# A float32 decoder layer on one core: feed-forward products from GpSimd to VectorE, compressed scores 64 columns wide, and other orders on VectorE and ScalarE

## Chip, core and metric

The kernel runs on one core of a Trainium2 chip. The metric is the time of one execution on the device in microseconds (us); the number compared is the median over runs. All arithmetic is float32 in and out. Where a matrix product needs full precision, each operand is split in two parts, `hi` (rounded to the fp32r form) and `lo` (the rest), and three fp32r products are added: lo by hi, hi by lo, hi by hi.

## What is computed

One decoder layer over 512 tokens of width 2048. The reference, cut to what matters:

```python
h = rms_norm(x, norm_mix)
proj = h @ w_in + b_in                       # q, k, v of two head groups, gates
# group A, 16 heads, three branches, mixed by sigmoid gates:
kc, vc = compress(k_c), compress(v_c)        # 31 compressed tokens per kv head (4 kv heads)
s_c = q @ kc.T * scale + bias;  p_c = masked_softmax(s_c);  o_c = p_c @ vc
o_s = attention over selected blocks         # here all 8 blocks: causal attention
o_w = attention over a window of 512
o_a = g0 * o_c + g1 * o_s + g2 * o_w
# group B, 16 heads: window of 128, one sink per head
x = x + concat(o_a, o_b) @ w_out
h = rms_norm(x, norm_ffn)
x = x + (silu(h @ w_gate) * (h @ w_up)) @ w_down      # width 5632
return rms_norm(x, norm_final)
```

## The kernel before

Each engine has its own instruction stream, written out by hand; engines wait for each other with counting semaphores (`pe.wait_ge(masked, n)` and the like), and the order within an engine is the order of the code. SyncE issues nearly all DMAs.

**Front, to about 230 us.** x is transposed, squared and split; `w_in` comes in units of 2048 columns through a ring. ScalarE makes the hi part of a unit (`split_hi`), VectorE the lo part (`split_lo`, line 1681), TensorE multiplies.

**Attention, about 230 to 600 us.** The work is a list of items: `c` is the compressed branch of two heads, `s` and `w` are the selected and the window branch of one head, `b` is a head of group B. There are 8 `c` items. The loop goes over x, and in step x TensorE does `score(x)`, `transpose_first(x-2)`, small pieces of `w_in` that fill the time (`mini`, lines 2876 to 2880), `transpose_third(x-2)` (line 2754) and `products(x-3)` (line 2784). VectorE adds the bias to the scores of x (`mask_scores`, line 1943, for `c` items lines 1911 to 1918), normalises x-1 (line 1977), makes lo parts of minis (1746), makes lo parts of the stacked queries and keys of the next round of four heads (`stack_lo_of`, line 1893, three steps of each round), and copies a third of the transposed probabilities of x-2 out of PSUM (`copy_third`, line 1987). `transpose_first` of a later step waits for that copy. In a `c` item TensorE makes 16 matmuls of 32 columns: for each of 4 token tiles and 2 heads one with `kc_lo` (line 2695) and one with `kc_hi` (2697), added up in PSUM. Item x+1 writes its fourth tile to bank 0 too, and waits there until `masked` says that the `c` item is fully masked.

**Behind attention, about 600 to 755 us.** The output projection: unit 0 to 3 of `w_out` (`out_unit`, lines 2797 to 2799), then three column groups by seven products of sums of quarters in place of eight (`out_piece`, line 2856). For these VectorE adds the sums S1 to S4 of the activations (`s_sum_of`, line 2049), and both engines split them (`s_hi_of` line 1387, `s_lo_of` line 2056). `waiting_hi` and `waiting_lo` (lines 1356 and 1992) split the rest of the attention output.

**The turn, about 755 to 775 us.** The new x is scaled and transposed on TensorE (`turn`, line 2923). The first quarter, B11, is raised by the norm's weights and split (`raise_b11` line 2225, `b11_lo_of` line 2238) and used by `first_piece` (line 2940). `out_c21(3)` adds the last tile of the projection (line 2098); the second half of `turn("B21")` waits for it.

**Feed-forward, about 770 us to the end.** Gate and up products run in 22 groups n (even: gate, odd: up) of 14 pieces of weights (1024 columns), again by seven products; TensorE takes them through lines 2989, 2992 and 2994. ScalarE makes a piece's hi part (1470), VectorE its lo part (2197); the ring holds 4 pieces. Between pieces VectorE adds weight quarters (lines 2326 to 2341) and gathers results from PSUM (2277 to 2298). For each pair of groups, a block, the gate's four quarters are multiplied by the up's: one of them on VectorE (`h11`), three on GpSimd (`up_times_gate`, line 1163); then four sums and differences of quarters (`h_add`, line 1169, GpSimd) are split by ScalarE (1594) and VectorE (`h_lo_of`, 2318) and stored. 10 blocks have 3 + 4 such GpSimd instructions, the last has 3. The down products follow from about 1600 us (lines 3041 to 3046).

## Time and profile before

| | |
|---|---|
| median of 3 runs | 2065.58 us (2061.4 to 2069.88) |
| profiled execution, its own time | 2062.77 us |
| its span, first to last instruction | 2061.1 us |
| TensorE busy | 2014.3 us, 98% |
| TensorE weight loads busy | 1815.4 us, 88% |
| VectorE busy | 1641.3 us, 80% |
| ScalarE busy | 988.6 us, 48% |
| GpSimd busy | 201.1 us, 10% |
| mean granted TensorE clock | 0.997 |

In the rows below a line is start, duration, engine, line of the code, operation, what it writes and reads, and in brackets the idle time just before it on its engine and what ended it. PE is TensorE, PEld its weight loads, DVE VectorE, ACT ScalarE, POOL GpSimd. Matmuls are pipelined, so that the duration of one is longer than the step from one start to the next.

### The profile page before, as it was taken

How to read it: one execution, taken by the hardware profiler on the slowest of the kernel's cores; microseconds unless marked ns; L12 is line 12 of the kernel's file. 1: busy time of each engine (PE TensorE's matmuls, PEld its weight loads, DVE VectorE, ACT ScalarE, POOL GpSimd, SP SyncE). 2: the span in 40 equal slices, each digit the busy share in tenths (PEclk: the TensorE clock that was granted, in tenths of full speed). 3: DMA queues.
4: the chain of work that ended last, by engine and by line, in shares of the span. 5: the costliest groups of instructions: out<-in, count | busy, mean ns of one | idle time of the engine just before them, and what ended most of it. 6: DMA issues, size and time to landing. Idle time of an engine off the chain costs nothing.

```text
span 2061.1 us, 33210 instructions
## 1 busy us (share of the span) xinstructions
PE 2014.3 (98%) x13637; PEld 1815.4 (88%) x13637; DVE 1641.3 (80%) x2226; ACT 988.6 (48%) x1515; POOL 201.1 (10%) x105
## 2 busy tenths in 40 slices
PE   8999999999989999999999999999999999999998
PEld 7888777777668999999999999999999988888886
DVE  6823567777768878889889888889889898989895
ACT  5212357667763566444444444444444433333343
POOL 4000000000000000302302302302302100000002
PEclk9999999999999999999999999999999999999999
DMA  7681212222025442454454454454454865655622
GB/s 267 205 227 56 68 57 57 65 65 58 30 98 189 145 152 94 144 174 154 144 179 148 149 179 143 144 178 150 144 172 164 310 218 179 239 210 165 245 102 82
DMA packets 211849, 306.52 MB, mean 149 GB/s; under 512 B 8881, under 2 KB 146161, under 8 KB 207089
## 3 DMA queue, kind: packets, MB, share of 16 engines
q1 hardware_dynamic: 211664, 304.38, 45.0%
q8 instruction: 108, 1.77, 0.4%
q14 instruction: 45, 0.36, 0.1%
q10 hardware_dynamic: 32, 0.01, 0.0%
HBM read 248.79 MB, written 55.57 MB: 148 GB/s over the span
## 4 chain that ended last, share of the span: by engine, by line
PE 92%; DVE 3%; issue 2%; ACT 2%; DMA 0%; POOL 0%; DVEq 0%; ACTq 0%; POOLq 0%
PE bank L2989 12%; PE bank L2994 12%; PE bank L2992 12%; PE bank L3044 6%; PE bank L3046 6%; PE bank L3041 6%; PE bank L2549 3%; PE bank L2551 3%; PE bank L2550 3%; PE bank L2715 3%; PE bank L2876 2%; PE bank L2880 2%; PE bank L2878 2%; PE bank L2784 2%; PE bank L2744 2%
## 5 line engine op out<-in xcount | busy, mean ns | idle before, releaser
L1470 ACT ACTIVATE w_all<-raw 128x1024 fp32r<-128x1024 f32 x292 | 305.6, 1058 | 269.6 <-PE bank L3046 156.9
L2197 DVE TENSOR_TENSOR w_all<-raw,w_all 128x1024 fp32r<-128x1024 f32 x292 | 383.2, 1325 | 64.4 <-ACT w_all L1470 64.0
L2989 PE MATMUL bank<-x_T,w_all 128*128 128x256 f32 x1344 | 374.4, 279 | 0.0
L2994 PE MATMUL bank<-x_T,w_all 128*128 128x256 f32 x1344 | 373.5, 278 | 0.0
L2992 PE MATMUL bank<-x_T,w_all 128*128 128x256 f32 x1344 | 373.5, 278 | 0.0
L2989 PE MATMUL bank<-x_B,w_all 128*128 128x256 f32 x1008 | 280.5, 278 | 0.9 <-DVE w_all L2197 0.8
L2992 PE MATMUL bank<-x_B,w_all 128*128 128x256 f32 x1008 | 279.7, 277 | 0.0
L2994 PE MATMUL bank<-x_B,w_all 128*128 128x256 f32 x1008 | 279.6, 277 | 0.0
L2989 PEld LDWEIGHTS bank<-x_T,w_all 128*128 128x128 f32 x1344 | 253.1, 188 | 0.9
L2994 PEld LDWEIGHTS bank<-x_T,w_all 128*128 128x128 f32 x1344 | 252.8, 188 | 0.0
L2992 PEld LDWEIGHTS bank<-x_T,w_all 128*128 128x128 f32 x1344 | 252.6, 188 | 0.0
L1470 ACT ACTIVATE w_all<-proj_q 128x1024 fp32r<-128x1024 f32 x150 | 158.5, 1060 | 183.2 <-PE bank L2994 113.4
L2197 DVE TENSOR_TENSOR w_all<-proj_q,w_all 128x1024 fp32r<-128x1024 f32 x150 | 182.9, 1221 | 56.4 <-ACT w_all L1470 56.1
L1163 POOL TENSOR_TENSOR proj_q<-proj_q 128x512 f32<-128x512 f32 x33 | 68.7, 2083 | 1337.8 <-DVE proj_q L2288 1309.3
L2989 PEld LDWEIGHTS bank<-x_B,w_all 128*128 128x128 f32 x1008 | 189.9, 188 | 2.1 <-DVE w_all L2197 1.6
L2994 PEld LDWEIGHTS bank<-x_B,w_all 128*128 128x128 f32 x1008 | 189.5, 188 | 0.0
L2992 PEld LDWEIGHTS bank<-x_B,w_all 128*128 128x128 f32 x1008 | 189.3, 188 | 0.0
L3041 PE MATMUL bank<-w_all,x_B 128*128 128x512 f32 x320 | 124.6, 389 | 0.0
L3044 PE MATMUL bank<-w_all,x_B 128*128 128x512 f32 x320 | 124.6, 389 | 0.0
L3046 PE MATMUL bank<-w_all,x_B 128*128 128x512 f32 x320 | 124.6, 389 | 0.0
L1681 DVE TENSOR_TENSOR w_all<-raw,w_all 128x2048 fp32r<-128x2048 f32 x19 | 43.5, 2290 | 83.6 <-ACT w_all L1206 83.5
L2549 PE MATMUL bank<-act_lo,w_all 128*128 128x512 f32 x272 | 108.0, 397 | 0.5 <-DVE w_all L1701 0.5
(333 smaller groups left out, 4531.7 us busy)
## 6 DMA issues: line engine op xcount, KB each, us to landing
raw<-in_w_gate SPq DMA_DIRECT2D x39, 1024.0 KB, 5.4
h_scratch<-late SPq DMA_DIRECT2D x70, 512.0 KB, 3.2
raw<-in_w_down SPq DMA_DIRECT2D x50, 512.0 KB, 5.2
proj_q<-in_w_up SPq DMA_DIRECT2D x22, 1024.0 KB, 7.0
raw<-in_w_up SPq DMA_DIRECT2D x22, 1024.0 KB, 8.0
x_B<-h_scratch SPq DMA_DIRECT2D x20, 1024.0 KB, 4.9
raw<-in_w_in SPq DMA_DIRECT2D x16, 1024.0 KB, 10.4
x_T<-h_scratch SPq DMA_DIRECT2D x15, 1024.0 KB, 7.5
```

What stands on the lines that cost most here:

```text
L1163: nc.gpsimd.tensor_tensor(quarter(f, t), up_stage, quarter(f, t), ALU.mult)\
L1470: nc.scalar.activation(piece_hi(p), piece_raw(n, k), ACT.Copy).then_inc(piece_hi_done, 1)
L2197: nc.vector.tensor_tensor(piece_lo(p), piece_raw(n, k), piece_hi(p).bitcast(F32), ALU.subtract).then_inc(piece_lo_done, 1)
L2549: nc.tensor.matmul(dst[c][:, :], wh[:, t, cs], x_lo(t), start=start, stop=False)
L2550: nc.tensor.matmul(dst[c][:, :], wl[:, t, cs], x_hi(t), start=False, stop=False)
L2551: done = nc.tensor.matmul(dst[c][:, :], wh[:, t, cs], x_hi(t), start=False, stop=stop)
L2989: nc.tensor.matmul(dst, wh[:, t, cs], x_lo(x)[:, cols], start=start and part == 0 and t == 0 and a == 0, stop=False, skip_group_check=True)
L2992: nc.tensor.matmul(dst, wl[:, t, cs], x_hi(x)[:, cols], start=False, stop=False, skip_group_check=True)
L2994: done = nc.tensor.matmul(dst, wh[:, t, cs], x_hi(x)[:, cols], start=False, stop=part == 1 and t == 3, skip_group_check=True)
L3041: nc.tensor.matmul(dst[:, :], h_lo, wh[:, t, :], start=start and part == 0 and t == 0, stop=False, skip_group_check=True)
L3044: nc.tensor.matmul(dst[:, :], h_hi, wl[:, t, :], start=False, stop=False, skip_group_check=True)
L3046: done = nc.tensor.matmul(dst[:, :], h_hi, wh[:, t, :], start=False, stop=part == 1 and t == 1, skip_group_check=True)
```

## The change

1. The seven GpSimd instructions of a block (`up_times_gate`, `h_add`) go to VectorE, at written places between its pieces. GpSimd keeps its work at the two ends of the kernel.
2. A `c` item's scores are made by 8 matmuls of 64 columns. The moving operand is `kc_hi` and `kc_lo` side by side, the results of the two stand apart in bank 0, and VectorE adds them: first the hi result and the bias as before, then one more instruction on 128x256 elements adds the lo result. The rest of the masking works in place on `prob_c`. Item x+1 now waits for the instruction that has read bank 0 last, and no longer for the last one of the item.
3. `copy_third` stands ahead of `stack_lo_of` on VectorE.
4. Behind attention, the splits of `w_out` units 2 and 3 stand ahead of the sums S1 to S4 and their splits, on both engines.
5. At the turn, `out_c21(3)` stands ahead of `b11_lo_of`. In the feed-forward part `c12` stands ahead of `h_lo_of(..., 1)`.

```diff
+        def kc_both(kv):
+            hi = kc_hi[:, kv, :]
+            return bass.AP(hi.tensor, hi.offset, [list(hi.ap[0]), [LO_AT, 2], list(hi.ap[1])])
...
 # GpSimd: the functions and this loop go
-            for block in range(FF_BLOCKS):
-                up_times_gate(block, c22_made, 1, 1)
-                up_times_gate(block, c12_made, 0, 1)
-                if block < LAST_BLOCK:
-                    pool.wait_ge(h_made, 3 * block + 2)
-                    pool.wait_ge(h11_made, block + 1)
-                    pool.wait_ge(h_lo_done, 7 * block + 2)
-                    h_add(block, 0, (1, 1), (0, 1), (1, 1), ALU.add)
...
 # ScalarE, behind attention
+            split_hi(OUT0 + 2)
             s_hi_of(0)
-            split_hi(OUT0 + 2)
             for t in range(3 * UNIT_KT, KT):
                 waiting_hi(t)
+            split_hi(OUT0 + 3)
             s_hi_of(1)
             s_hi_of(2)
-            split_hi(OUT0 + 3)
...
 # VectorE, mask_scores of a c item
-                    ps = banks[0][:, 0:256].rearrange("p (i h c) -> p i h c", i=TT, h=2)
+                    ps = banks[0][:, :].rearrange("p (i h s c) -> p i h s c", i=TT, h=2, s=2)
+                    both = prob_c[:, :, h % 4:h % 4 + 2, :]
...
-                    then(nc.vector.tensor_reduce(least, score_c, AX.X, ALU.min))
+                    nc.vector.tensor_tensor(both, score_c, ps[:, :, :, 1, :], ALU.add)\
+                      .then_inc(masked, 1)
+                    dve.wait_ge(masked, 4 * x + 3)
+                    then(nc.vector.tensor_reduce(least, both, AX.X, ALU.min))
...
 # VectorE, attention loop
+                if 2 <= x <= N_ITEMS + 1 and ITEMS[x - 2][0] in "sw":
+                    copy_third(x - 2)
                 if x in STACK_STEP:
                     stack_lo_of(*STACK_STEP[x])
-                if 2 <= x <= N_ITEMS + 1 and ITEMS[x - 2][0] in "sw":
-                    copy_third(x - 2)
...
 # VectorE, feed-forward
+            def up_times_gate(block, made, f, t):
+
+                dve.wait_ge(made, 2 * block + 1)
+                dve.wait_ge(gate_silu, 4 * block + 4)
+                nc.vector.tensor_tensor(quarter(f, t), up_stage, quarter(f, t), ALU.mult)\
+                  .then_inc(h_made, 1)
...
                     if k == 1 and n > 1:
+                        c12(n - 1)
                         if not up:
+                            up_times_gate(block - 1, c12_made, 0, 1)
                             h_lo_of(block - 1, 1)
-                        c12(n - 1)
+                            h_add(block - 1, 0)
+                    if k == 2 and not up:
+                        h_add(block - 1, 1)
+                        h_add(block - 1, 2)
                     if k == 3 and n > 1:
                         c21(n - 1)
+                        if not up:
+                            up_times_gate(block - 1, c21_made, 1, 0)
+                    if k == 8 and not up:
+                        h_add(block - 1, 3)
...
                         c22(n)
+                        if up:
+                            up_times_gate(block, c22_made, 1, 1)
...
 # TensorE, score(x) of a c item
-                            at = 64 * i + 32 * e
-                            nc.tensor.matmul(banks[0][:, at:at + 32], queries(h + e, i),
-                                             kc_lo[:, h // 4, :], start=True, stop=False)
-                            last = nc.tensor.matmul(banks[0][:, at:at + 32], queries(h + e, i),
-                                                    kc_hi[:, h // 4, :], start=False, stop=True)
+                            at = P * i + 64 * e
+                            last = nc.tensor.matmul(banks[0][:, at:at + 64], queries(h + e, i),
+                                                    kc_both(h // 4), start=True, stop=True)
...
-                        pe.wait_ge(masked, 4 * x)
+                        pe.wait_ge(masked, 4 * (x - 1) + 3)
```

VectorE in step x of a `b` item, before: the lo parts of the stacks (`w_all<-proj_q`, `w_all<-proj_kv`) stand between the mini's lo part and the copy of the third (`raw<-bank`).

```order
293 L1746 TENSOR_TENSOR mini_lo<-mini_raw,mini_hi 128x512
294 L1893 SCALAR_TENSOR_TENSOR w_all<-proj_q,w_all 64x512
295 L1893 SCALAR_TENSOR_TENSOR w_all<-proj_kv,w_all 64x512 x2
296 L1987 COPY raw<-bank 128x256
297 L1943 ISA proj_kv,stats<-bank,w_all,sink_sb 128x128
```

The same place of the changed kernel: the copy comes first.

```order
295 L1720 TENSOR_TENSOR mini_lo<-mini_raw,mini_hi 128x512
296 L1964 COPY raw<-bank 128x256
297 L1867 SCALAR_TENSOR_TENSOR w_all<-proj_q,w_all 64x512
298 L1867 SCALAR_TENSOR_TENSOR w_all<-proj_kv,w_all 64x512 x2
299 L1920 ISA proj_kv,stats<-bank,w_all,sink_sb 128x128
```

VectorE behind attention, before. `w_all<-raw` 128x2048 are the lo parts of `w_out` units 2 and 3, `act_lo<-proj_q` the lo parts of the attention output, the rest the sums S and their lo parts.

```order
953 L1992 TENSOR_TENSOR act_lo<-proj_q,act_hi 128x512 x4
954 L2049 TENSOR_TENSOR x_plain_T<-proj_q 128x2048
955 L2049 TENSOR_TENSOR x_plain_B<-x_plain_T,proj_q 128x2048
956 L1681 TENSOR_TENSOR w_all<-raw,w_all 128x2048
957 L1992 TENSOR_TENSOR act_lo<-proj_q,act_hi 128x512 x4
958 L2049 TENSOR_TENSOR x_plain_B<-proj_q,x_plain_B 128x2048
959 L2056 TENSOR_TENSOR x_T<-x_plain_T,x_T 128x2048
960 L2049 TENSOR_TENSOR work<-proj_q 128x2048
961 L2056 TENSOR_TENSOR x_B<-x_plain_B,x_B 128x2048
962 L1681 TENSOR_TENSOR w_all<-raw,w_all 128x2048
```

And now: unit 2 has one sum ahead of it where two stood, and between the second `act_lo` group and unit 3 stands one sum, where four instructions stood.

```order
961 L1969 TENSOR_TENSOR act_lo<-proj_q,act_hi 128x512 x4
962 L2026 TENSOR_TENSOR x_plain_T<-proj_q 128x2048
963 L1655 TENSOR_TENSOR w_all<-raw,w_all 128x2048
964 L1969 TENSOR_TENSOR act_lo<-proj_q,act_hi 128x512 x4
965 L2026 TENSOR_TENSOR x_plain_B<-x_plain_T,proj_q 128x2048
966 L1655 TENSOR_TENSOR w_all<-raw,w_all 128x2048
967 L2033 TENSOR_TENSOR x_T<-x_plain_T,x_T 128x2048
```

VectorE in a gate group of the feed-forward part, before, from the up group's `c22` (row 1139) over pieces 13, 0, 1, 2 and 3 (`w_all<-` 128x1024).

```order
1139 L2288 TENSOR_TENSOR proj_q<-proj_q,bank 128x512
1140 L2197 TENSOR_TENSOR w_all<-proj_q,w_all 128x1024
1141 L2197 TENSOR_TENSOR w_all<-raw,w_all 128x1024
1142 L2318 TENSOR_TENSOR late<-proj_q,late 128x512
1143 L2293 TENSOR_TENSOR proj_q<-proj_q,bank 128x512
1144 L2197 TENSOR_TENSOR w_all<-raw,w_all 128x1024 x2
1145 L2331 TENSOR_TENSOR raw<-raw 128x2048
1146 L2298 TENSOR_TENSOR proj_q<-proj_q,bank 128x512
1147 L2318 TENSOR_TENSOR late<-proj_q,late 128x512
1148 L2197 TENSOR_TENSOR w_all<-raw,w_all 128x1024
```

The same stretch now, behind `c22` and its product (L2289) and piece 13: the product and three sums (L2306) by piece 2, one more product by piece 3.

```order
1157 L2174 TENSOR_TENSOR w_all<-raw,w_all 128x1024
1158 L2270 TENSOR_TENSOR proj_q<-proj_q,bank 128x512
1159 L2289 TENSOR_TENSOR proj_q<-proj_q 128x512
1160 L2318 TENSOR_TENSOR late<-proj_q,late 128x512
1161 L2306 TENSOR_TENSOR proj_q<-proj_q 128x512
1162 L2174 TENSOR_TENSOR w_all<-raw,w_all 128x1024
1163 L2306 TENSOR_TENSOR proj_q<-proj_q 128x512 x2
1164 L2174 TENSOR_TENSOR w_all<-raw,w_all 128x1024
1165 L2331 TENSOR_TENSOR raw<-raw 128x2048
1166 L2275 TENSOR_TENSOR proj_q<-proj_q,bank 128x512
1167 L2289 TENSOR_TENSOR proj_q<-proj_q 128x512
1168 L2318 TENSOR_TENSOR late<-proj_q,late 128x512
```

Seven instructions are added in each such stretch of 28 pieces, five of them between piece 0 and piece 3.

## Rows read from the trace of the kernel before

**Rows 1.** The page, busy time, share and count of each engine.
```profile
PE 2014.3 (98%) x13637; PEld 1815.4 (88%) x13637; DVE 1641.3 (80%) x2226; ACT 988.6 (48%) x1515; POOL 201.1 (10%) x105
```

**Rows 2.** Windows: length, busy PE, PEld, DVE, ACT, POOL, clock, DMA share, GB/s.
```profile
549.00:578.00 29.00, 21.72 (x134) 13.98 (x133) 25.54 (x93) 24.24 (x63) 0.00 (x0) 0.96 0.01 2
763.60:766.40 2.80, 2.69 (x13) 2.69 (x14) 0.76 (x6) 2.19 (x6) 0.00 (x0) 0.50 0.53 175
766.00:1600.00 834.00, 833.10 (x7232) 831.03 (x7232) 721.69 (x583) 404.27 (x471) 161.23 (x70) 1.00 0.48 156
```

**Rows 3.** Waits of TensorE: us in total, times, longest.
```profile
PE bank L2744 <- issue: 6.8, 4, 2.4
PE bank L2730 <- issue: 4.2, 2, 3.0
...
PE bank L2797 <- DVE w_all L1681: 3.3, 2, 2.3
PE bank L2923 <- DVE x_plain_T L2098: 3.3, 1, 3.3
...
PE bank L2989 <- DVE w_all L2197: 0.8, 1, 0.8
```

**Rows 4.** Timeline, TensorE: first score of a c item, and what follows it.
```profile
237.53 0.18 PE L2695 MATMUL bank<-w_all 128*128 128x32 f32 x1
...
239.23 0.47 PE L2876 MATMUL bank<-act_lo,mini_hi 128*128 128x512 f32 x1
```

**Rows 5.** One line's instructions, 64 columns wide: durations min/median/max, first and last start.
```profile
L2626 PE MATMUL bank<-proj_q,proj_kv x16: 275/275/323, 209.5 to 211.2; 128*128 128x64 f32 x16
```

**Rows 6.** Timeline around copies of the third, VectorE and TensorE.
```profile
326.84 0.38 PE L2754 MATMUL bank<-ident,proj_kv 128*128 128x128 f32 x2
...
327.86 1.41 DVE L1893 SCALAR_TENSOR_TENSOR w_all<-proj_kv,w_all 64x512 fp32r<-64x512 f32 x2 [0.52 <-ACT w_all L1268]
...
329.30 0.42 DVE L1987 COPY raw<-bank 128x256 f32<-128x256 f32 x1
...
329.82 0.95 PE L2744 MATMUL bank<-ident,prob_x 128*128 128x128 f32 x7 [1.66 <-issue]
...
559.14 0.63 PE L2730 MATMUL bank<-ident,raw 128*128 128x128 f32 x4 [1.15 <-issue]
...
569.20 1.06 PE L2744 MATMUL bank<-ident,prob_x 128*128 128x128 f32 x8 [1.12 <-issue]
```

**Rows 7.** Timeline behind attention, VectorE's lo parts of units 2 and 3.
```profile
615.43 2.29 DVE L1681 TENSOR_TENSOR w_all<-raw,w_all 128x2048 fp32r<-128x2048 f32 x1 [1.47 <-ACT w_all L1206]
...
628.86 2.29 DVE L1681 TENSOR_TENSOR w_all<-raw,w_all 128x2048 fp32r<-128x2048 f32 x1
```

**Rows 8.** Timeline at the turn, VectorE and TensorE.
```profile
760.70 2.36 DVE L2238 TENSOR_TENSOR x_B<-x_plain_T,x_B 128x1024 fp32r<-128x1024 f32 x2 [1.12 <-ACT x_B L1538]
762.98 0.68 DVE L2098 TENSOR_TENSOR x_plain_T<-proj_q,bank 128x512 f32<-128x512 f32 x1
...
763.71 1.97 PE L2923 MATMUL bank<-ident,proj_q 128*128 128x128 f32 x8 [3.29 <-DVE x_plain_T L2098]
...
765.33 0.56 PE L2940 MATMUL bank<-x_B,w_all 128*128 128x256 f32 x1
```

**Rows 9.** Timeline of one gate group's start, VectorE and TensorE.
```profile
1238.06 2.36 DVE L2197 TENSOR_TENSOR w_all<-raw,w_all 128x1024 fp32r<-128x1024 f32 x1 [1.25 <-ACT w_all L1470]
1240.35 3.38 DVE L2331 TENSOR_TENSOR raw<-raw 128x2048 f32<-128x2048 f32 x1
...
1245.35 2.31 DVE L2197 TENSOR_TENSOR w_all<-raw,w_all 128x1024 fp32r<-128x1024 f32 x1
...
1247.71 0.39 PE L2989 MATMUL bank<-x_T,w_all 128*128 128x256 f32 x1
...
1248.18 1.21 DVE L2197 TENSOR_TENSOR w_all<-raw,w_all 128x1024 fp32r<-128x1024 f32 x1
```

**Rows 10.** Groups of GpSimd's instructions: busy us, mean ns, idle before them.
```profile
L1169 POOL TENSOR_TENSOR proj_q<-proj_q 128x512 f32<-128x512 f32 x40 | 99.0, 2474 | 75.4 <-DVE late L2318 73.0
```

More of the change, by code:

```diff
@@ L1910, in mask_scores @@
                                       [list(tab.ap[0]), [SEQ, 2], [CMP_STRIDE, n]])
-                        last = nc.vector.tensor_tensor(score_c[:, i, :, 0:n], ps[:, i, :, 0:n], tab,
-                                                       ALU.add)
-                        if i < TT - 1:
+                        last = nc.vector.tensor_tensor(score_c[:, i, :, 0:n], ps[:, i, :, 0, 0:n],
+                                                       tab, ALU.add)
+                        if i < 2:
                             last.then_inc(masked, 1)
@@ L1916, in mask_scores @@
                     least = cstats[:, 0, :].rearrange("p (i h) -> p i h", i=TT)
-                    then(nc.vector.tensor_reduce(least, score_c, AX.X, ALU.min))
+                    nc.vector.tensor_tensor(both, score_c, ps[:, :, :, 1, :], ALU.add)\
+                      .then_inc(masked, 1)
+                    dve.wait_ge(masked, 4 * x + 3)
+                    then(nc.vector.tensor_reduce(least, both, AX.X, ALU.min))
                     nc.vector.tensor_tensor(
-                        prob_c[:, :, h % 4:h % 4 + 2, :],
-                        least.unsqueeze(3).to_broadcast([P, TT, 2, 32]), score_c, ALU.subtract)\
+                        both, least.unsqueeze(3).to_broadcast([P, TT, 2, 32]), both, ALU.subtract)\
                       .then_inc(masked, 1)
@@ L2150, in _ @@
             s_sum_of(0)
-            s_sum_of(1)
             split_lo(OUT0 + 2)
@@ L2154, in _ @@
                 waiting_lo(t)
+            s_sum_of(1)
+            split_lo(OUT0 + 3)
+            s_lo_of(0)
             s_sum_of(2)
-            s_lo_of(0)
+            s_lo_of(1)
             s_sum_of(3)
-            s_lo_of(1)
-            split_lo(OUT0 + 3)
             s_lo_of(2)
@@ L2306, in h11, with h_add @@
                   .then_inc(h11_made, 1)
+            def up_times_gate(block, made, f, t):
[3 more added lines that the diff above has]
+                  .then_inc(h_made, 1)
+            def h_add(block, k):
+                if block or k:
+                    dve.wait_ge(h_sum, 4 * block + k)
+                if k == 0:
+                    dve.wait_ge(h_made, 3 * block + 2)
+                    dve.wait_ge(h11_made, block + 1)
+                    dve.wait_ge(h_lo_done, 7 * block + 2)
+                elif k == 3:
+                    dve.wait_ge(h_made, 3 * block + 3)
+                    dve.wait_ge(h_lo_done, 7 * block + 6)
+                dst, a, b, op = (((1, 1), (0, 1), (1, 1), ALU.add), ((0, 1), (0, 0), (0, 1), ALU.subtract),
+                                 ((0, 0), (1, 1), (0, 0), ALU.subtract),
+                                 ((1, 0), (1, 0), (0, 0), ALU.subtract))[k]
+                nc.vector.tensor_tensor(quarter(*dst), quarter(*a), quarter(*b), op).then_inc(h_sum, 1)
             def h_lo_of(block, j):
@@ L2372, in _ @@
             raise_b11()
+            out_c21(3)
             b11_lo_of(0)
             b11_lo_of(1)
-            out_c21(3)
             row_mean_of(1)
@@ L2465, in _ @@
                             c12(LAST_UP)
+                            up_times_gate(LAST_BLOCK, c12_made, 0, 1)
                         if k == 3:
                             c21(LAST_UP)
+                            up_times_gate(LAST_BLOCK, c21_made, 1, 0)
                             h_lo_of(LAST_BLOCK, 2)
```

18 lines of the change are left out of this document (removed).

## The prediction

> **What bounds the kernel now.** I read the busy times first. TensorE is busy for 98% of the span [rows 1], and in the gate and up products for 833.10 of 834 us, weight loads for 831 of them, at a granted clock of 1.00 [rows 2]. Nothing that VectorE gains there can shorten more than the few tenths that TensorE waits. So the gain has to come from two places: matmuls that are no longer issued, and TensorE's waits elsewhere. The span less busy time is 2061.1 - 2014.3 = 46.8 us, the ceiling for all waits together. The table of TensorE's waits says which of these the change can touch [rows 3]: six waits of transposes put down to "issue", 6.8 + 4.2 = 11.0 us; two of `out_unit` for VectorE's split of `w_out`, 3.3 us; one of `turn` for line 2098, 3.3 us; one for a piece's lo part, 0.8 us. Together 18.4 us. The third thing to see is where VectorE is itself nearly full: at the end of attention, where the minis have run out, it is busy 25.54 of 29 us while TensorE is busy 21.72 [rows 2].
>
> **Part 1, the compressed scores.** The 16 matmuls of an item start at 237.53 and the next other matmul starts at 239.23, so they hold TensorE for 1.70 us, 0.106 each [rows 4]. What does a 64 column matmul cost? The nearest row is line 2626, also 64 columns with a weight load before each: 15 steps from 209.5 to 211.2, 0.113 us each [rows 5]. Eight of them are 0.91 us, so an item saves 0.79, and eight items 6.3 us. The ends: nothing, if the price went by the number of columns, which the 0.106 for 32 and 0.113 for 64 speak against; and 6.8, if eight took exactly half of 1.70. VectorE gets one instruction more per item, 128x256 elements with one operand in PSUM. Its nearest row is the copy of the same size from PSUM, 0.42 us [rows 6]; eight are 3.4 us. It is hidden by TensorE's minis in seven items, and its release of bank 0 comes earlier by one instruction, which about pays it back for the next item.
>
> **Part 2, the third copied first.** Look at the timeline around 329 [rows 6]. The transposes of the third start at 326.84 and are done by about 327.2. VectorE could copy then, but stands before the stacks: it waits 0.52 us for ScalarE and works for 1.41, and copies at 329.30. TensorE starts its next transposes 0.1 us behind that copy's end, after 1.66 us of idleness. "issue" in the table hides this: the releaser is the copy. With the copy first, it is done by about 327.6, before TensorE gets there, and the whole 1.66 us goes. The six waits are of this kind. What a wait can give is the stack work that stood in front of its copy: 1.41 us for two stacks, 2.1 for three (3 x 0.70), more where ScalarE was waited for. Against the waits that means: the longest, 3.0, keeps 1.6 and gives 1.4; the 2.4 gives 2.1 or a little more; the other four, 11.0 - 3.0 - 2.4 = 5.6, go whole. Sum 9.1 us. The ends are 5 (half of it comes back as a wait on ScalarE, whose copies are next in line) and 11.0. The stacks come 0.35 to 0.42 later and are wanted only a step or more later.
>
> **Part 3, behind attention.** TensorE waited 1.0 and 2.3 us for the lo parts of units 2 and 3, which VectorE made at 615.43 and 628.86 [rows 3, 7]. In the new order one 2.29 us sum moves behind unit 2, and the 1.47 us that VectorE waited for ScalarE's split of it go too, as that split no longer stands behind one that waits for a sum: 3.8 us sooner. Between units 2 and 3 stand three instructions of 2.29 fewer, 6.9 us on top. Both exceed the waits, 3.3 us go. What is late next are the sums S and their splits; the first product that needs one comes after unit 3, 11 us later, and its slack I read as 3 us or more. Ends: 2.0 and 3.3.
>
> **Part 4, the turn.** VectorE was idle for 1.12 us before 760.70, waiting for ScalarE, and the moved instruction takes 0.68 [rows 8]: it fits in the gap and costs the split nothing. TensorE was idle from 760.42 to 763.71. Now its transposes run through to about 761.4; then the first matmul of line 2940 needs the first half of the split, done about 761.9. It starts at 761.9 and not at 765.33: 3.4 us. In 763.60 to 766.40 the granted clock was 0.50, the lower level of 1.2 GHz, following the idle stretch [rows 2]. If TensorE isn't idle there, the matmuls from 765.33 to 766.40 take half of that 1.07 us, another 0.5. Sum 3.9; ends 2.5 and 4.5.
>
> **Part 5, the feed-forward part.** Seven instructions per block, 73 in all, move to VectorE. Their form is 128x512 with both operands in SBUF; the nearest row is line 2098, as large and with one operand in PSUM, 0.68 us [rows 8]. The other side is what GpSimd does to VectorE. While GpSimd works, line 2197 takes 2.36 and 2.31 us, and just after 1.21 [rows 9]; line 2331, of the size of the 2.29 us instructions of [rows 7], takes 3.38 there. These three alone lose 1.15 + 1.09 + 1.10 = 3.3 us up to piece 3. The five new instructions up to there, each 0.68 and, as a guess of mine, 0.04 for waiting on the one before, add 3.6. Beyond that, 1.25 us of idleness ahead of 1238.06 can be used. So piece 3, whose lo part ends at 1247.66 and which TensorE takes at 1247.71, with nothing to spare, comes sooner by about 1 us. I take the 0.8 us of the one listed wait as the gain; ends: +9 (below) and -2.
>
> The Trainium skill (GPSIMD Engine Reference, Key points) says of elementwise work that VectorE is structurally about twice as fast as GpSimd. GpSimd's instruction takes 2.474 us here [rows 10]; by that page of the Trainium skill the moved one would take about 1.24 on VectorE (an estimate), where the row of the twin says 0.68. By the row VectorE's added work is 73 x 0.68 = 50 us, by the page of the skill 73 x 1.24 = 90 us. What the page's price would do is a rival below.
>
> **The sum.** 6.3 + 9.1 + 3.3 + 3.9 + 0.8 = 23.4 us. From that I take 1.5: in the stretch 549 to 578, where VectorE is 88% busy [rows 2], stand two of the six waits, 1.15 and 1.12 [rows 6], and one `c` item's 0.8, 3.1 in all, and I let half of it turn into other waits, since there VectorE's own work sets the pace. The forecast is 22 us off the profiled execution's own 2062.77, 2040.8. The median of the runs shown, 2065.58, is 2.8 above that execution; 22 off the median gives 2043.6, which I round to 2043.5. What a measurement can't tell from no change is about 0.5%, 10 us.
>
> **Rivals.**
> *A, the forecast*: -22, with its own range -17 to -29. The far end has all ends of parts 2 to 4 (2.5 more), the 2 of part 5, no loss in the last stretch (1.5), and part of a low-clock stretch less. Chance 0.64.
> *B, VectorE and ScalarE take the attention gain back*: they are near TensorE's pace, so that an earlier start of TensorE ends in a wait for a copy of ScalarE or a mask of VectorE. For it speak 549 to 578; against it that in the 329 us example [rows 6] both engines have work ready that TensorE's earlier start lets them begin earlier. Half of parts 1 and 2 is lost (7.7): about -13, 2052. Chance 0.22.
> *C, the feed-forward part becomes VectorE's*, the one on the other side. The place is piece 3 of a gate group, 10 times, where there is no slack. If what GpSimd costs VectorE were not given back, 3.6 us of new work less 1.25 of idleness puts TensorE 2.3 us late per group, 23 in all: 2067, the same. If an instruction moreover costs 1.24 as by half of GpSimd's 2.474 [rows 10], five are 6.5 with their waits, and without give-back 5.2 late per group, 52 in all: 2096. It turns slower than before once a group loses over 2.2 us, and slower by 0.5% at 3.2. With the give-back of 3.3 but the price of 1.24, piece 3 is late by 6.5 - 3.3 - 1.25 = 1.9: 19 in all, 2063. Chance 0.05 for slower, 0.05 for about the same. The page of the Trainium skill named above, with its factor of two, would make of it that last case.
> *D, a matmul of 64 columns costs twice one of 32*, so that part 1 gives nothing: -16, 2050. Chance 0.04, in the range of A and B.
>
> So faster by over 0.5%: A, D and most of B, 0.86; within 0.5%: the rest of B and half of C, 0.09; slower 0.05. The range: A's far end and a little more, -31, is 2034.5; B's near end, -10, is 2055.5. It leaves out C and the tails.
>
> **What would show it.** Right: eight matmuls of 128x64 per `c` item, 0.11 us apart; the "issue" waits of transposes down from 11.0 to about 2; no waits of line 2797's successor and of `turn` for VectorE; clock of 1.00 around 763; line 2174 (the old 2197) at 1.22 everywhere, VectorE's busy time in the feed-forward part unchanged or a few us lower; TensorE's busy time in 766 to 1600 still the whole stretch. Wrong: new TensorE waits for line 2174 at pieces 1 to 5 of gate groups (C); waits for ScalarE's copies (lines 1344, 1334) in attention that grow by as much as the others fall (B).

## The result, and the profile after

The changed kernel takes 2038.0 us (median of 5 runs, 2036.8 to 2039.7) where the kernel before takes 2065.6: a ratio of 0.9874, interval 0.9860 to 0.9889. The forecast was 2043.5. The profiled execution has 2038.37 us of its own for 2062.77 before, 24.4 us less; the forecast was 22.

The page's busy line of the changed kernel, beside [rows 1]:

```profile
PE 2001.5 (98%) x13573; PEld 1804.0 (89%) x13573; DVE 1637.4 (80%) x2307; ACT 983.2 (48%) x1515; POOL 34.0 (2%) x32
```

There are 64 matmuls fewer, and GpSimd's 73 instructions are gone. VectorE has 81 instructions more and is busy 3.9 us less.

TensorE's waits in the changed kernel (us in total, times, longest), beside [rows 3]:

```profile
PE bank L2765 <- ACT raw L1318: 5.7, 6, 2.1
...
PE bank L2708 <- DVE w_all L1867: 2.2, 1, 2.2
...
PE bank L2741 <- issue: 1.6, 1, 1.6
...
PE bank L2755 <- issue: 1.0, 2, 0.9
PE bank L2934 <- ACT x_plain_T L1473: 0.7, 1, 0.7
PE bank L2951 <- DVE x_B L2215: 0.7, 1, 0.7
```

The "issue" waits of transposes are down from 11.0 to 2.6 us, and those of the output units and of `turn` for VectorE are gone. Two have grown: for ScalarE's copies in attention (line 2765; 4.2 us in a profile of the kernel before) and for a stack's lo part (line 2708; 1.6 before).

Where the time went is read from stage lengths: the distance between the first matmul of one function and the first of the next. "Stops" are the steps of 0.15 us and more between two matmuls of the up stage, less the ordinary 0.113 each, in how many places. Each row is one profiled execution.

| profile | attention | output units | pieces, turn | first piece | up stage | its stops | span |
|---|---|---|---|---|---|---|---|
| before | 356.2 | 60.4 | 123.1 | 49.2 | 812.7 | 4.3 in 17 | 2061.1 |
| before, again (e11) | 354.4 | 60.4 | 123.1 | 49.0 | 815.8 | 5.0 in 17 | 2061.1 |
| changed | 343.4 | 56.6 | 121.5 | 48.7 | 805.7 | 1.0 in 2 | 2036.3 |
| changed, again (e12) | 343.3 | 56.6 | 121.5 | 49.9 | 806.0 | 0.4 in 1 | 2037.3 |
| e1, part 5 alone | 354.4 | 60.4 | 123.1 | 47.9 | 806.1 | 1.1 in 4 | 2053.4 |
| e2, parts 1 to 4 | 343.4 | 56.6 | 120.0 | 48.7 | 811.3 | 5.0 in 19 | 2040.1 |
| e5, part 1 alone | 350.1 | 60.4 | 123.1 | 48.2 | 808.9 | 5.1 in 21 | 2051.3 |
| e6, part 2 alone | 349.4 | 60.4 | 123.1 | 47.9 | 809.5 | 5.8 in 21 | 2049.5 |
| e7, stacks sooner | 342.5 | 56.6 | 120.0 | 48.7 | 804.5 | 1.0 in 2 | 2032.2 |
| e8, two late pieces | 343.5 | 56.6 | 119.8 | 48.7 | 803.5 | none | 2032.3 |
| e9, parts 3 and 4 | 356.4 | 56.7 | 120.4 | 49.9 | 810.6 | 5.1 in 21 | 2052.3 |
| e10, improved | 339.9 | 56.6 | 119.8 | 48.7 | 803.9 | none | 2029.7 |

The down stage takes 433.7 to 434.1 in all of them. So of the 24.8 us of span, attention gave 12.8, the output units 3.8, the stretch with the turn 1.6, the first piece 0.5, the up stage 7.0; the front was 0.9 longer. The front's 0.9 isn't the change's work: the changed kernel's profile has a stretch at clock 0.50 from 52.1 us on, which the first profile of the kernel before lacks. In the profiles that have this stretch the front takes 226.2 to 227.4 us, in the four that lack it 224.6 to 225.7.

The changed kernel's compressed scores, timeline of TensorE, beside [rows 4]; and the added VectorE instruction (durations min/median/max, starts):

```profile
238.49 0.97 PE L2708 MATMUL bank<-w_all 128*128 128x64 f32 x8
239.30 0.48 PE L2887 MATMUL bank<-act_lo,mini_hi 128*128 128x512 f32 x1
```
```profile
L1892 DVE TENSOR_TENSOR raw<-work,bank x8: 420/421/422, 240.6 to 538.0; 128x256 f32<-128x256 f32 x8
```

Eight matmuls hold TensorE for 0.81 us, where 16 held it for 1.70; the new instruction takes 0.42.

At the turn the transposes follow on each other's heels, and the first matmul of `first_piece` waits only for the lo part, as forecast:

```profile
745.47 2.03 PE L2934 MATMUL bank<-ident,proj_q 128*128 128x128 f32 x16
748.15 0.35 PE L2951 MATMUL bank<-x_B,w_all 128*128 128x256 f32 x1 [0.66 <-DVE x_B L2215]
```

### The profile page after: what moved, and what is told of

It reads as the page before. It is cut to its first block, busy times and chain, and to the rows that moved or that the text cites. A ratio compares the mean times of both kernels' runs of the same rounds, so it can differ in the third digit from the quotient of the medians.

```text
span 2036.3 us, 33090 instructions
## 1 busy us (share of the span) xinstructions
PE 2001.5 (98%) x13573; PEld 1804.0 (89%) x13573; DVE 1637.4 (80%) x2307; ACT 983.2 (48%) x1515; POOL 34.0 (2%) x32
## 4 chain that ended last, share of the span: by engine, by line
PE 89%; DVE 5%; ACT 3%; issue 2%; DMA 2%; SPq 0%; DVEq 0%; ACTq 0%
PE bank L3000 12%; PE bank L3003 12%; PE bank L3005 12%; PE bank L3052 6%; PE bank L3055 6%; PE bank L3057 6%; PE bank L2562 3%; PE bank L2563 3%; PE bank L2564 3%; PE bank L2726 3%; PE bank L2887 2%; PE bank L2891 2%; PE bank L2889 2%; PE bank L2795 2%; PE bank L2755 2%
## 5 line engine op out<-in xcount | busy, mean ns | idle before, releaser
L2174 DVE TENSOR_TENSOR w_all<-raw,w_all 128x1024 fp32r<-128x1024 f32 x292 | 352.3, 1220 | 49.7 <-ACT w_all L1444 49.3
L1444 ACT ACTIVATE w_all<-proj_q 128x1024 fp32r<-128x1024 f32 x150 | 158.7, 1060 | 190.6 <-PE bank L3005 123.1
L2563 PE MATMUL bank<-act_hi,w_all 128*128 128x512 f32 x272 | 106.8, 392 | 0.0
```

The costliest lines, as they stand in the source:

```text
L1444: nc.scalar.activation(piece_hi(p), piece_raw(n, k), ACT.Copy).then_inc(piece_hi_done, 1)
L2174: nc.vector.tensor_tensor(piece_lo(p), piece_raw(n, k), piece_hi(p).bitcast(F32), ALU.subtract).then_inc(piece_lo_done, 1)
L2563: nc.tensor.matmul(dst[c][:, :], wl[:, t, cs], x_hi(t), start=False, stop=False)
```

## The feed-forward part: experiments 1 to 4

The forecast had this part at -0.8; the table's up stage is 7 us shorter. Four kernels ask where that comes from.

**e1, part 5 alone; e2, everything but part 5.** In e1 the kernel before gets only this (and the same for the other six instructions of a block, and `c12` ahead of `h_lo_of(..., 1)`):

```diff
-                nc.gpsimd.tensor_tensor(quarter(f, t), up_stage, quarter(f, t), ALU.mult)\
+                nc.vector.tensor_tensor(quarter(f, t), up_stage, quarter(f, t), ALU.mult)\
```

e2 is the changed kernel with it undone.

> Part 5 alone on the kernel before: the seven GpSimd instructions of a block on VectorE, c12 ahead of h_lo. The prediction priced it at -0.8 us (2064.8 against 2065.6). The trace of the changed kernel shows the gate and up stage 6.9 us shorter. Theory V (moving the work off GpSimd gives all of it: VectorE's lo parts are on time and the waits go): 2058.5, -7, with the gate and up stage 6.9 us shorter. Rival R (most of the 6.9 us is a difference between one run and the next, or comes from another part): -0.8 to -3, 2063 to 2065.

> Parts 1 to 4 alone; the feed-forward part as in the kernel before, with GpSimd. Theory V: 2045.5, which is 7 us over the changed kernel's 2038, and a gate and up stage as long as before. Rival R: 2039 to 2041. The prediction's terms for parts 1 to 4, less its 1.5, give -21.1 on 2065.6, 2044.5; the landmarks of the changed kernel (12.7 in attention, 3.8 behind it, 2.2 about the turn) give -18.7, 2046.9.

e1: 2058.2 us, ratio 0.9969 (0.9958 to 0.9981). e2: 2043.5, ratio 0.9903 (0.9884 to 0.9922). The two add up to the whole, and the part is worth 5.5 to 6.3 us by the medians; e1's interval alone allows 3.9 to 8.7, more than rival R's 3 at most. That is theory V. The waits table can't show it. Here is a place in the second profile of the kernel before (e11), TensorE at piece 5 of a gate group:

```profile
1253.15 0.28 PE L2992 MATMUL bank<-x_B,w_all 128*128 128x256 f32 x1
1253.26 0.28 PE L2994 MATMUL bank<-x_B,w_all 128*128 128x256 f32 x1
1253.49 0.39 PE L2989 MATMUL bank<-x_B,w_all 128*128 128x256 f32 x1
1253.71 0.28 PE L2992 MATMUL bank<-x_B,w_all 128*128 128x256 f32 x1
1253.83 0.28 PE L2994 MATMUL bank<-x_B,w_all 128*128 128x256 f32 x1
```

No bracket, so no idle time: a matmul lasts 0.28 and the next normally starts 0.11 behind it, so a step of 0.23 hides inside the one before. But two steps of 0.23 and 0.22 cost 0.22 us, and the matmul that waited is marked by its duration, 0.39. This stands at piece 3 or piece 5, or both, of every gate group: 17 places, 4.3 us, of which the table lists one, 0.8 [rows 3].

Behind many of these stops the profile has a second thing. Windows of the same execution (length, busy PE, PEld, DVE, ACT, POOL, clock, DMA share, GB/s):

```profile
1254.00:1301.00 47.00, 47.00 (x401) 47.00 (x401) 38.61 (x32) 21.53 (x24) 3.29 (x1) 1.00 0.46 150
1302.00:1330.00 28.00, 28.00 (x248) 28.00 (x248) 25.60 (x20) 12.65 (x16) 13.90 (x6) 1.00 0.48 162
```

Same work, clock 1.00 in both, but 47.00/401 = 0.117 us a matmul against 28.00/248 = 0.113. Such stretches take 5.0 us of the first profile's up stage and some 7 of the second's; in e5 and e6, with the old feed-forward part too, there are none. So they are no fixed cost, and the up stage of the kernel before has 809 to 816 us. Over the profiles in the table it is 811.5 with GpSimd (six) and 805.6 with the change's own feed-forward part (four: changed, e12, e1, e7): 5.9 less, 4.2 of it stops (5.1 against 0.9 in the mean).

**e3, GpSimd works beside.** The changed kernel, with GpSimd busy at the 73 old places, four times each:

```diff
+                for s, count in paces:       # the semaphores that paced GpSimd before
+                    pool.wait_ge(s, count)
+                    for part in range(4):
...
+                        nc.gpsimd.tensor_tensor(ones[:, :], ident[:, :], ident[:, :], ALU.mult)\
```

> The changed kernel, and GpSimd works beside it in the gate and up stage: at each of the 73 old places four products of 128x128 elements from two operands in SBUF, into a buffer that nothing reads. VectorE's own work stays. If GpSimd's traffic stretches VectorE's instructions with two operands in SBUF (contention, theory V): line 2174 back to a mean of about 1.32 us, and since VectorE now has the seven instructions too, piece 3 comes 2 to 3 us late in each of 10 gate groups: +20 to +30, 2058 to 2068. If the stretch in the kernel before came from something else than GpSimd's traffic (its waits for VectorE's results, say): line 2174 stays at 1.22, and the time within 2 us of 2038.

2065.2 us, 27 more than the changed kernel: theory V. Of the profile's 29.7 us, 27.7 are in the up stage. Its groups of VectorE and GpSimd, and its longest wait of TensorE:

```profile
L2192 DVE TENSOR_TENSOR w_all<-raw,w_all 128x1024 fp32r<-128x1024 f32 x292 | 366.9, 1270 | 48.4 <-ACT w_all L1462 48.0
...
L2293 DVE TENSOR_TENSOR proj_q<-proj_q,bank 128x512 f32<-128x512 f32 x21 | 14.2, 678 | 0.3 <-PE bank L3023 0.3
```
```profile
L1176 POOL TENSOR_TENSOR ones<-ident 128x128 f32<-128x128 f32 x292 | 304.3, 1042 | 1286.2 <-DVE proj_q L2307 1255.6 <-DVE proj_q L2324 6.3
```
```profile
PE bank L3018 <- DVE w_all L2192: 20.8, 21, 1.3
```

GpSimd shares no buffer that VectorE uses there, and still the lo parts take 1.27 us in the mean (1.34 to 1.43 where one starts while GpSimd works). That is less than forecast (1.32): these small instructions stretch VectorE's less than the 128x512 ones did. An instruction with one operand in PSUM (`bank`) isn't touched, 678 ns. The same pair in the kernel before (e11) and in the changed one:

```profile
L2197 DVE TENSOR_TENSOR w_all<-raw,w_all 128x1024 fp32r<-128x1024 f32 x292 | 379.8, 1313 | 65.9 <-ACT w_all L1470 65.5
...
L2331 DVE TENSOR_TENSOR raw<-raw 128x2048 f32<-128x2048 f32 x10 | 33.8, 3382 | 0.0
```
```profile
L2174 DVE TENSOR_TENSOR w_all<-raw,w_all 128x1024 fp32r<-128x1024 f32 x292 | 352.3, 1220 | 49.7 <-ACT w_all L1444 49.3
...
L2289 DVE TENSOR_TENSOR proj_q<-proj_q 128x512 f32<-128x512 f32 x33 | 22.9, 693 | 1.1
...
L2331 DVE TENSOR_TENSOR raw<-raw 128x2048 f32<-128x2048 f32 x10 | 22.8, 2284 | 0.0
```

How the two engines hold each other up can be read from single instructions of the kernel before:

```profile
1231.03 1.22 DVE L2197 TENSOR_TENSOR w_all<-proj_q,w_all 128x1024 fp32r<-128x1024 f32 x1
...
1231.19 2.21 POOL L1163 TENSOR_TENSOR proj_q<-proj_q 128x512 f32<-128x512 f32 x1 [50.78 <-DVE proj_q L2288]
...
1232.62 1.86 DVE L2197 TENSOR_TENSOR w_all<-raw,w_all 128x1024 fp32r<-128x1024 f32 x1 [0.37 <-ACT w_all L1470]
```

GpSimd's instruction starts 0.16 us behind VectorE's and ends at 1233.40, 1.15 behind the end of VectorE's at 1232.25. VectorE's next one starts inside it and ends at 1234.48, 1.08 behind GpSimd's end, where alone it takes 1.22. So the one that comes second waits for the first and then still needs nearly its whole time. It is so all over the stage: 55 of the 73 GpSimd instructions end 1.15 to 1.16 us behind the end of the VectorE instruction that they found running. All 63 VectorE instructions that took longer than alone started while GpSimd worked, and the 32 lo parts among them end 1.08 or 1.09 us behind GpSimd's end. Together the 63 lose 57.0 us, more than the 73 moved instructions cost at 0.69 each (50). GpSimd's own time is in this line of the kernel before (min/median/max):

```profile
L1169 POOL TENSOR_TENSOR proj_q<-proj_q x40: 1286/2268/3292, 853.6 to 1565.0; 128x512 f32<-128x512 f32 x40
```

1.29 us is what the eight take that started just ahead of VectorE's; the rest of the 2.47 in [rows 10] is waiting for VectorE.

By the Trainium skill (SBUF — State Buffer, section "Who interferes with whom") a VectorE instruction with two SBUF inputs contends with a GpSimd one that reads SBUF, and one with at most one SBUF input, outside the 2-port modes, doesn't. Rows agree on both. It also calls the pair of ports that the two share an exclusive lock, and the trace agrees with that too (1.15 and 1.08 us behind the other's end).

**e4, VectorE's slack.** Each moved instruction is preceded by another that it waits for:

```diff
+            def twice(q):
+                nc.vector.tensor_tensor(q, q, q, ALU.max).then_inc(again, 1)
+                extra.append(1)
+                dve.wait_ge(again, len(extra))
```

> The changed kernel, and each of the 73 moved VectorE instructions is preceded by one of the same size (the maximum of a quarter with itself, in place, both operands in SBUF) that it waits for; the output is unchanged. It prices VectorE's slack: five more by piece 3 of a gate group are 3.6 us. The trace of the changed kernel has some 1.6 us of slack there: 2 us late per gate group, +20, 2058, with waits of TensorE for line 2174's successor. If VectorE had 3.6 us of slack: +0 to 2. If none, +36, and rival C of the prediction would have been near: 2074.

2085.5 us, 47.5 more than the changed kernel; all three guesses were too low. Of the profile's 49.4 us, 46.0 are in the up stage and 2.6 in attention, which this edit doesn't touch. TensorE at one piece 3, and a window behind another such stop:

```profile
1015.43 0.38 PE L3010 MATMUL bank<-x_T,w_all 128*128 128x256 f32 x1 [2.32 <-DVE w_all L2175]
```
```profile
851.40:856.90 5.50, 5.50 (x27) 5.50 (x27) 5.50 (x6) 3.82 (x6) 0.00 (x0) 0.50 0.47 178
```

The step at piece 3 is 2.60 us in nearly every gate group, 2.5 more than it should be: about 1.1 of the added 3.6 was slack. With piece 8, late in three groups, the 14 long steps of the up stage cost 29.6 us. Another 11 are 110 matmuls 0.213 us apart, at clock 0.50, the lower level, behind some of the stops; TensorE had been idle for 3.0 us before the first of these stretches and for 2.3 before the six others, but three more stops of 2.3 had none behind them. So lateness is paid a second time. Rival C's mechanism is real, and its price per late us was set too low.

## Attention: experiments 5 to 7

**e5, part 1 alone:**

```diff
-                            nc.tensor.matmul(banks[0][:, at:at + 32], queries(h + e, i),
-                                             kc_lo[:, h // 4, :], start=True, stop=False)
+                            last = nc.tensor.matmul(banks[0][:, at:at + 64], queries(h + e, i),
+                                                    kc_both(h // 4), start=True, stop=True)
```

> Part 1 alone on the kernel before: a c item's scores as 8 matmuls of 64 columns. Theory A (the prediction's term): TensorE's 0.79 us an item all arrive at the end, -6.3, 2058 against 2064.4. Rival B (VectorE's added instruction and the pace of VectorE and ScalarE take part of it): -3 to -4, 2061, with longer waits of the transposes.

2054.6 us, ratio 0.9953 (0.9941 to 0.9965), 9.7 less. Attention is 6.1 shorter than in the first profile, as theory A says; the other 3.8 of the profile's 9.8 is the up stage without its slower stretches, which this part doesn't touch. That the timed runs owe their surplus to the same is likely, not shown. The ledger closes: eight times 1.70 - 0.81 is 7.1, and the "issue" waits grew from 11.0 to 12.0, since what TensorE saved ahead of a copy that came no sooner (278.54) it spent waiting for it.

**e6, part 2 alone:**

```diff
+                if 2 <= x <= N_ITEMS + 1 and ITEMS[x - 2][0] in "sw":
+                    copy_third(x - 2)
                 if x in STACK_STEP:
                     stack_lo_of(*STACK_STEP[x])
-                if 2 <= x <= N_ITEMS + 1 and ITEMS[x - 2][0] in "sw":
-                    copy_third(x - 2)
```

> Part 2 alone on the kernel before: the copy of the third ahead of the stacks' lo parts. Theory A: -9.1, 2055.3, the waits put down to issue from 11.0 to about 2. Rival B: the waits go, but waits for ScalarE's copies and for a round's last stack take part of them back at the round change near 500 and behind 549: in the changed kernel's trace these new waits are about 2.2 and 2.1 us, so -5 to -6, 2059.

2055.7 us, ratio 0.9959 (0.9945 to 0.9973), 8.5 less; attention is 6.8 shorter. Both theories had a part. In its waits "issue" is down to 1.8 us, but these have come:

```profile
PE bank L2754 <- ACT raw L1344: 5.7, 6, 2.1
...
PE bank L2695 <- DVE w_all L1893: 2.2, 1, 2.2
```

1.5 and 0.6 us more than before: 9.2 - 2.1 = 7.1. The two places in the changed kernel, ScalarE and TensorE:

```profile
502.27 1.28 ACT L1242 ACTIVATE w_all<-proj_kv 64x512 fp32r<-64x512 f32 x2
...
551.80 0.57 ACT L1323 ACTIVATE proj_q<-bank 128x512 f32<-128x512 f32 x1
552.28 1.06 ACT L1318 ACTIVATE raw<-bank 128x512 f32<-128x512 f32 x2
```
```profile
505.05 1.08 PE L2708 MATMUL bank<-w_all 128*128 128x64 f32 x8 [2.18 <-DVE w_all L1867]
...
552.91 0.44 PE L2765 MATMUL bank<-ident,proj_kv 128*128 128x128 f32 x2 [2.06 <-ACT raw L1318]
```

At 505 the first item of a round wants its stacks, whose last part only came in the step before. At 552 ScalarE has worked without a gap since 543.36, and its copy comes last in that queue.

The granted clock is a term that this ledger leaves out. Right behind these two waits, the changed kernel's windows show it at 0.50, the lower level:

```profile
506.10:509.50 3.40, 3.40 (x13) 3.01 (x13) 3.16 (x14) 1.80 (x4) 0.00 (x0) 0.50 0.03 5
553.90:557.30 3.40, 3.40 (x13) 2.35 (x10) 2.52 (x6) 3.35 (x11) 0.00 (x0) 0.50 0.03 7
```

Attention has three such stretches in the changed kernel (the third from 564.1 on) and in e6, two in e5 and in the first profile of the kernel before (from 295.6 and 575.5), and one in e11. What one costs shows behind the wait of 3.04 us, which both profiles of the kernel before have: from there to the products of the same step it is 5.36 us in the first, at 0.50, and 3.75 in e11, at 1.00. So new waits can also lose clock, and the 1.8 us between the two profiles' attention is mostly this one stretch. Against e11, e5 is worth 4.3 us in attention, e6 5.0 and the whole change 11.0.

**e7, stacks sooner** tries to take these two away:

```diff
-STACK_STEP = {first_item(r) - STACK_PARTS - (r != 3) + part: ...
+STACK_STEP = {first_item(r) - STACK_PARTS - (r != 3) - (r == 7) + part: ...
...
+                early = STACK_STEP.get(x) == (3, STACK_PARTS - 1)
+                if early:
+                    stack_hi_of(*STACK_STEP[x])
                 for m in minis_of(x + 1):
                     mini_hi_of(m)
```

and the same for `stack_lo_of` ahead of `normalise`.

> The changed kernel, with the stacks of two rounds sooner: the last part for round 3 ahead of the mini's hi part on ScalarE and ahead of the normalising on VectorE, and the three parts for round 7 each one step earlier. If the leak in attention is that the stacks stand ahead of what TensorE wants next (the wait of 2.18 us near 505 and the waits for ScalarE's copies of 2.06, 0.69 and 0.69 behind 541): the first falls by 1.3, the others by 2 or more, and each of the half-clock stretches behind them may go: -3 to -5, 2034. If ScalarE's and VectorE's whole load sets the pace there, the waits only move: within 1 of 2038.

2035.3 us, ratio 0.9862 (0.9850 to 0.9875), 2.7 below the changed kernel; but attention is only 0.9 shorter, below the 3 to 5 expected for a cure. The wait at 505 went from 2.2 to 1.7 and the one at 552 from 2.1 to 1.6. VectorE now stood for 1.6 us waiting for ScalarE's hi parts: both lo parts of the keys need both hi parts. The order in the last step wasn't the limit, ScalarE's load up to it was. (The rest of the profile's 4.1 is the turn stretch and the up stage, see next.)

## Behind attention, and an improved version: experiments 8 to 12

**e8, two late pieces.** In the changed kernel TensorE stops for 0.4 us at 649, for a piece's lo part that stands behind the last of the sums S. Earlier, VectorE has 1.90 us of idleness. And piece 8 of a gate group was late twice.

```diff
+                    if g == 1 and k == 4:
+                        s_lo_of(3)
                     out_piece_lo(g, k)
...
-                    if g == 1 and k == 6:
-                        s_lo_of(3)
...
-                    if k == 8 and not up:
+                    if k == 7 and not up:
                         h_add(block - 1, 3)
```

> The changed kernel, with two lo parts on time: behind attention the last lo part of the sums S, in VectorE's 1.9 us of idleness ahead of piece 4, and in the feed-forward part the fourth h_add one piece earlier. TensorE's short stops at 649 (0.41 us) and at piece 8 of gate groups (0.5 us, two times) should go: -1.5. If a short stop also brings on the stretch of slower steps seen behind it (118 ns a matmul for 113, 1.6 us behind the stop at 649 and about 1.2 behind the one at 857): -3 to -4, 2034.5. If these stretches come without a stop, -1.5 at most, and steps of 118 ns remain behind 649.

2034.3 us, ratio 0.9855 (0.9841 to 0.9870). All stops are gone, and so are the slower steps; the same window in e12 (first) and e8:

```profile
651.00:700.00 49.00, 49.00 (x422) 49.00 (x421) 43.38 (x41) 24.23 (x35) 0.00 (x0) 1.00 0.51 163
```
```profile
651.00:700.00 49.00, 49.00 (x433) 49.00 (x433) 43.21 (x41) 24.95 (x35) 0.00 (x0) 1.00 0.50 158
```

Eleven more matmuls in the same time, a gain of 1.2 us. It speaks for a stop that brings on slow steps. But it isn't proof: stops of 0.4 to 0.5 us at this place had the slow stretch behind them in the changed kernel, in e12 and e3, while stops of 0.2 in e2 and e7 and of 0.6 and 0.8 in e9 and e4 had not. And e10, which has no stop either, has slower steps in its up stage: 173 matmuls from 840 to 860 us, where e8 has 177.

**e9, parts 3 and 4 alone:**

```diff
+            split_hi(OUT0 + 2)
             s_hi_of(0)
-            split_hi(OUT0 + 2)
...
+            out_c21(3)
             b11_lo_of(0)
             b11_lo_of(1)
-            out_c21(3)
```

> Parts 3 and 4 alone on the kernel before: the orders behind attention and at the turn. The prediction's terms: -3.3 and -3.9, -7.2 in all, 2057. Taken from the traces so far: output units 3.8 shorter, the turn 3.1 shorter with 0.6 behind it, -7.5; against it, a new stop of 0.2 to 0.4 us near 664 for a late lo part, with at worst 1.6 us of slower steps behind it.

2057.3 us, ratio 0.9968 (0.9955 to 0.9982): 6.6 less by the ratio, 8.5 by the medians. The units are 3.7 us shorter and the stretch with the turn 2.7, with a stop of 0.6 us at 671 in it.

**e10, combined:** e8, the stacks of round 7 a step earlier, and for round 3:

```diff
-            per = -(-count // STACK_PARTS)
+            per = 4 if r == 3 else -(-count // STACK_PARTS)
```

> The version with e8's two edits and the stacks of round 7 one step earlier; for round 3, instead of the new order in its last step, all parts in the first two steps (4 and 4 in place of 3, 3 and 2). From e8 (2034.3): if round 3's stacks are then on time, the wait of 2.2 near 505 goes, and with 0.4 at 552: -2.5, 2032. If ScalarE, which has no gap from 494 to 505, only passes the 1.3 us on as later copies: as e8 with -0.8, 2033.5, or no better than e8.

2030.2 us (2029.5 to 2034.0), ratio 0.9838 (0.9816 to 0.9860): 35 us off the kernel before by the medians, 33 by the ratio, and all of its runs below all of the changed kernel's, though these are from another set of runs. TensorE at round 3's first item:

```profile
503.68 1.05 PE L2708 MATMUL bank<-w_all 128*128 128x64 f32 x8 [0.31 <-DVE stats L1920]
```

The wait of 2.2 us is gone, and attention is 3.5 shorter than in the changed kernel, more than the wait: the clock is 1.00 behind it, where the changed kernel's is 0.50, and by the products that follow another 1.3 us is gained. ScalarE could take the 1.3 us a step earlier; e10's second theory falls.

**e11 and e12**, both kernels profiled again:

> The kernel before, profiled once more. In the first profile six stretches of its gate and up stage ran at 117 to 118 ns a matmul, 5.0 us more than at 113.3; in the two profiles with the old feed-forward part of the same chip job as this kind of run (e5, e6) there were none. If the stretches come and go between executions, this profile has another set of them or none, the short stops at pieces 3 and 5 of the ten gate groups are there as before (4 to 5 us), and its gate and up stage is 809 to 813 us.

> The changed kernel, profiled once more: gate and up stage 804 to 806 us, at most four short stops (1.0 us), with the slower steps behind the stop at 649 (1.6 us) or without.

The table has both. e12 is as expected; e11's up stage is above the 809 to 813 us expected and the longest of all, with five stretches of slower steps, each behind a stop or at the stage's start; so the first profile's 812.7 is no unlucky outlier. e11's attention is 1.8 below the first one's (the clock, above); so differences of 2 us between two profiles mean nothing by themselves.

## Why the prediction was right, step by step

- **What bounds the kernel**: right, but for one sentence. "Nothing that VectorE gains there can shorten more than the few tenths that TensorE waits" failed: the table of waits has only idle time, and 4 to 5 us of stops in the up stage lay below what it can see.
- **Part 1, -6.3**: 6.1 arrived (e5; 4.3 against e11, whose attention has one stretch of low clock less). The 64 column matmul was priced about right (0.113 forecast, so 0.91 for eight; 0.81 measured), and 1.0 of 7.1 turned into wait.
- **Part 2, -9.1**: 6.8 (e6), inside the ends of 5 and 11. The "issue" waits went as read, one by one. What the sum left out is what gives back 2.1: ScalarE's copies, next in line (1.5), which the prediction had only in its near end, and a round's last stack (0.6). "Wanted only a step or more later" failed there: TensorE already waited 1.6 us for that stack before. The clock behind the new waits wasn't in the sum at all. The 1.5 taken off in the sum for such a leak was the right idea for a place (behind 549) that turned out to be ScalarE's and not VectorE's. Together the two parts were 15.4, 13.9 with the leak taken off, and 12.8 came: 2.6 were lost where rival B had 7.7, so rival B was there with a third of its size. (B's "about -13" doesn't follow from its own terms, which give 22 - 7.7 = 14.3.)
- **Part 3, -3.3**: the units gave 3.8, and 1.7 (121.5 - 119.8 of e8) went again, in both profiles of the changed kernel, for what was "late next": the slack of "3 us or more" for the sums held, but their lo part pushed a piece's lo part over its time (e8). Most of the 1.7 is the slower steps behind that stop; in e2 and e7, where they didn't come, it is 0.2.
- **Part 4, -3.4 and -0.5**: the stretch gave 3.3 (e8 and e10 against before). The clock of 0.50 around 763 is gone, but no half a us can be seen for it: the first piece has 47.9 to 49.9 us with and without the change.
- **Part 5, -0.8, ends +9 and -2**: the step that failed. -5.5 to -6.3 came. The mechanism was right in all its parts: line 2174 at 1.22 everywhere, the moved instructions at 0.69, VectorE's busy time in the whole up stage 697 us against 702 with 73 instructions more, piece 3 late before and with about 1.1 us of slack after (e4). The size was wrong, because "I take the 0.8 us of the one listed wait" priced 17 stops by the one that the table lists. The rows had shown such a stop [rows 9]: the lo part ends at 1247.66 and TensorE starts at 1247.71 with a duration of 0.39. It had been read as "nothing to spare"; it was already late.
- **The factor of two** of the Trainium skill (GPSIMD Engine Reference, Key points) was applied to the wrong number. The mean of 2474 ns [rows 10] is about half waiting for VectorE. By GpSimd's own 1.29 us against 0.69 the factor is 1.9, and the trace agrees with the page. Half of 1.29 is 0.64, close to what the moved instructions take; so the price of 1.24, and the 6.5 us per group that rival C made of it, came from a duration that contained the contention already.
- The sum, -22 forecast against -24.4, is close partly by luck, since errors met: between the two profiles the up stage gave 6.2 more than said, attention 1.1 less, part 3 1.2 less, and the front was 0.9 longer.

## What to carry to other kernels

Where matmuls overlap, don't take the table of waits for all waits: look at the steps between starts at the first matmul of each buffer, and at its duration; a step of two is a wait, times the number of loops. When one engine's delay is removed, look up which engine is next in line at that very place, and how full it is. A GpSimd instruction in a stage that VectorE paces can cost VectorE time even if they share no data, so moving it over may cost VectorE nothing at all: here 50 us of work came and 57 us of waiting went. Before a duration is used as a price, look at the shortest of its kind: the mean can hold the wait that one wants to remove.

## What the hardware showed that was not expected

- A 128x512 instruction of GpSimd took 1.29 us when it started ahead of VectorE's, and 1.15 us from the end of a VectorE instruction with two operands in SBUF that it found running; VectorE's 128x1024 ones took 1.22 alone and 1.08 from GpSimd's end. With one operand in PSUM VectorE's took 0.68 in both cases.
- At a granted clock of 1.00 a matmul of 256 columns took 0.113 us in some stretches and 0.117 in others, for 6 to 68 us at a time, often but not always from a short stop on, and in other places from one execution to the next. What sets it is open.
- In the up stage, an idle stretch of 3.0 us and six of nine of 2.3 were followed by matmuls at clock 0.50, 11 us of loss in all (e4); idle stretches of up to 1.3 us were not (e3). In attention, the wait of 3.04 us was followed by clock 0.50 in one profile of the kernel before and by 1.00 in the other.
